# Recurrent gates in four stacked products, weights in a buffer of their own, zero fills spread evenly

## The reference

```python
proj = x @ w_in                                  # B | C | V_A | V_B | G, 512 channels each
y_a = B * conv3(C * V_A)
xc  = conv4(V_B) + bias
r   = sigmoid(einsum('bthi,hij->bthj', xh, wa) + ba)     # xh: xc as 8 heads x 64
i   = sigmoid(einsum('bthi,hij->bthj', xh, wx) + bx)
a   = exp(-8 * r * softplus(-lam)); b = sqrt(1 - a*a) * (i * xc)
h_t = a_t * h_(t-1) + b_t                         # over time
y_b = h * gelu(G)
x1  = layer_norm(alpha * x + concat(y_a, y_b) @ w_out)
y   = layer_norm(alpha * x1 + top-2-of-16 experts(x1))
```

## Time and profile before

| what | value |
|---|---|
| executions timed | 1200.48, 1204.1, 1204.4 us; median 1204.1 |
| the profiled execution | 1197.2 us, of which the span of its instructions is 1195.5 |
| PE busy | 1120.3 us (94% of the span) |
| DVE busy | 808.3 us (68%) |
| ACT busy | 538.6 us (45%) |
| POOL busy | 186.4 us (16%) |
| granted TensorE clock, mean | 0.977 of full speed |

### The profile page before, as it was taken

How to read it: one execution, slowest core, us unless ns; L and a number is a source line. 1 busy time by engine, 2 the same in 40 slices (tenths; PEclk the granted TensorE clock), 3 DMA queues, 4 the chain that set the end, 5 groups by cost and what they waited for, 6 DMA issues and landing times.

```text
span 1195.5 us, 20533 instructions
## 1 busy us (share of the span) xinstructions
PE 1120.3 (94%) x5736; PEld 996.2 (83%) x5737; DVE 808.3 (68%) x1532; ACT 538.6 (45%) x703; POOL 186.4 (16%) x189
## 2 busy tenths in 40 slices
PE   6999999999999999999999988899998999999970
PEld 6999999999999999878888867677887887878750
DVE  5666644465446546767777758797755898888874
ACT  4465433543354336422233312655544676656530
POOL 1000000010001000102222223406101031222222
PEclk9999999999999999999999989899999999999995
DMA  5431368788989454534444225896866789888563
GB/s 188 131 104 50 107 92 121 90 141 128 122 97 133 193 221 164 186 129 159 156 159 141 106 93 184 284 345 219 281 233 240 283 309 369 304 294 293 197 225 143
DMA packets 87274, 221.58 MB, mean 185 GB/s; under 512 B 19152, under 2 KB 45808, under 8 KB 80944
## 3 DMA queue, kind: packets, MB, share of 16 engines
q1 hardware_dynamic: 57824, 129.90, 34.6%
q0 software_dynamic: 18160, 59.53, 15.4%
q10 hardware_dynamic: 11232, 31.47, 13.3%
HBM read 133.75 MB, written 87.11 MB: 185 GB/s over the span
## 4 chain that ended last, share of the span: by engine, by line
PE 71%; DVE 9%; DMA 7%; issue 5%; ACT 4%; DVEq 2%; ACTq 1%; SPq 0%; POOL 0%; POOLq 0%
PE ps_va_b L293 14%; PE ps_vb_c L293 14%; PE ps_h L1488 9%; PE ps_vb_c L907 8%; PE ps_g L293 7%; PE ps_va_b L907 7%; PE ps_o L1466 5%; DMA gate<-g_scr 3%; PE ps_x L1455 2%; PE ps_r_i L302 2%; PE ps_r_i L920 1%; DVE w_lo_p L1658 1%; ACT x_hi L1116 1%; PE ps_h L1517 1%; DMA w_raw<-in_w_out 1%
## 5 line engine op out<-in xcount | busy, mean ns | idle before, releaser
L1488 PE MATMUL ps_h<-x_hi,xt_hi 128*128 x312 | 125.6, 403 | 2.2 <-issue 1.7
L293 PE MATMUL ps_vb_c<-x_hi,w_hi 128*128 (+1 forms) x320 | 114.4, 358 | 9.3 <-DVE x_lo L469 9.3
L1488 PE MATMUL ps_h<-x_hi,xt_lo 128*128 x312 | 121.9, 391 | 0.0
L1488 PE MATMUL ps_h<-w_lo,xt_hi 128*128 x312 | 121.6, 390 | 0.0
L293 PE MATMUL ps_vb_c<-x_hi,w_lo 128*128 (+1 forms) x320 | 113.9, 356 | 0.0
L293 PE MATMUL ps_vb_c<-x_lo,w_hi 128*128 (+1 forms) x320 | 113.2, 354 | 0.0
L293 PE MATMUL ps_va_b<-x_hi,w_lo 128*128 (+1 forms) x320 | 112.7, 352 | 0.0
L293 PE MATMUL ps_va_b<-x_hi,w_hi 128*128 (+1 forms) x320 | 112.6, 352 | 0.0
L293 PE MATMUL ps_va_b<-x_lo,w_hi 128*128 (+1 forms) x320 | 111.8, 349 | 0.0
L543 DVE TENSOR_TENSOR b_t<-a_t 128x420 f32<-128x420 f32 x20 | 11.9, 596 | 95.3 <-ACT a_t L387 95.3
L1121 DVE TENSOR_TENSOR w_lo<-x_hi_p,x_hi 128x2048 f32 (+1 forms) x30 | 68.5, 2288 | 8.5 <-ACT x_hi L1116 6.8
(11 more groups left out here) (361 smaller groups left out, 2680.6 us busy)
## 6 DMA issues: line engine op xcount, KB each, us to landing
x_hi_p<-in_w SPq DMA_DIRECT2D x48, 1024.0 KB, 7.4
o_scr<-x_raw ACTq DMA_DIRECT2D x42, 512.0 KB, 4.9
w_lo_p<-xs_scr SPq DMA_DIRECT2D x41, 512.0 KB, 5.9
o_scr<-w_lo_p SPq DMA_DIRECT2D x41, 512.0 KB, 6.2
w_raw<-in_w_in POOLq DMA_DIRECT2D x19, 512.0 KB, 4.6
xs_scr<-x_raw ACTq DMA_DIRECT2D x18, 512.0 KB, 6.6
x_raw<-in_x_t SPq DMA_DIRECT2D x20, 416.0 KB, 3.4
x_hi_p<-y_scr SPq DMA_DIRECT2D x16, 512.0 KB, 4.3
```

What stands on the lines that cost most here:

```text
L293: mm = pe.matmul(ps[i][:, 0:CHUNK], w[:, i, k], x[:, k, bass.ds(c * CHUNK, CHUNK)], start=(k == 0 and n == 0), stop=(k == KT - 1 and n == 2))
L1488: mm = pe.matmul(ps_h[par][:], x[:, par, k], w[:, bass.ds(at, 1), k].rearrange("p o n -> p (o n)"), start=(k == 0 and n == 0), stop=(k == ...
```

## The change

It has four parts. First, the gates' products: `xc_hi` and `xc_lo` give way to one tile `xc_st` of two slices, one for each head. A slice holds the 64 high rows of its head in one half of the partitions and the 64 low rows in the other. The weights of a slice hold r's block beside i's, and both again below, so a matmul of 128 rows gives hi+lo times the weights, for r and i of one head. With the weights' high and low part that is two matmuls per head, four in all. Head 0's r and i stand in the low and high half of one bank (`ps_ri`), head 1's i and r in those of the other (`ps_ir`); so `xc_hi`, `xc_lo` and the two Tanh become two instructions each, on 64 partitions. Second, the gates' weights come as six pieces instead of one, and for groups 1 to 3 into `l_raw`, columns 1024 to 1279 of `x_raw`, at the head of POOL's loop over the group before. Third, the zero fills: groups 1 and 2 issue seven per step in another order, their last steps five, group 3 four. Fourth, in group 0 every step awaits x by pieces, and SP's late x loads stand between the stores of `y_a` and `y_b`.

```diff
@@ -112,8 +113,7 @@
     xc = sb("xc", [P, LRU_N])
-    xc_hi = sb("xc_hi", [P, LRU_N], F32R)
-    xc_lo = sb("xc_lo", [P, LRU_N], F32R)
+    xc_st = sb("xc_st", [P, 2, LRU_N], F32R)
     ya = sb("ya", [P, EXT + 1])
@@ -127,15 +127,18 @@
     sp_t = sb("sp_t", [P, 8, GROUPS])
-    zero = x_raw[:].rearrange("p a b c -> p (a b c)")[:, 0:D]
+    zero, l_raw = (x_raw[:].rearrange("p a b c -> p (a b c)")[:, a:b] for a, b in ((0, D), (D, D + 2 * P)))
+    l_raw = l_raw.rearrange("p (k n) -> p k n", n=P)
...
     ps_g = ctx.enter_context(nc.psum_tensor("ps_g", [P, 512], F32))
-    ps_vb, ps_c, ps_va, ps_b, ps_r, ps_i = (t[:, i] for t in (ps_vb_c, ps_va_b, ps_r_i) for i in range(2))
+    ps_vb, ps_c, ps_va, ps_b, ps_ri, ps_ir = (t[:, i] for t in (ps_vb_c, ps_va_b, ps_r_i) for i in range(2))
+    low, high = slice(0, HALF), slice(HALF, P)
     ps = [ps_vb, ps_c, ps_va, ps_b, ps_g]
-    mag = ps_r[:, 0:LRU_N]
+    mag = ps_ri[:, 0:LRU_N]
@@ -197,6 +201,14 @@
+    def load_gates(pool, group, to):
+        gate = lambda rows, g, n: w_lru[group, rows, g:g + n, rows].rearrange("o p k n -> p (o k) n")
+        for rows in (low, high):
+            pool.dma_start(to[rows, 0].rearrange("p (k n) -> p k n", n=HALF), gate(low, 0, 2)).then_inc(s_lraw, 16)
+            for g in range(2):
+                pool.dma_start(to[rows, 1:2, (1 - g) * HALF:(2 - g) * HALF], gate(high, g, 1)).then_inc(s_lraw, 16)
     def mix_gpsimd(pool):
@@ -204,18 +216,18 @@
                 pool.wait_ge(s_wlo, i - 1)
-            dst = w_raw[:, i % 2] if i < MT else w_raw[:, i % 2, 0:2]
-            src = w_in[i] if i < MT else w_lru[0]
-            pool.dma_start(dst, src).then_inc(s_wraw[i % 2], 16)
+            if i < MT:
+                pool.dma_start(w_raw[:, i % 2], w_in[i]).then_inc(s_wraw[i % 2], 16)
+            else:
+                load_gates(pool, slice(0, 1), w_raw[:, 1, 0:2])
         with pool.Fori(1, GROUPS) as j:
-            for i in range(WP):
+            for i in range(MT):
                 pool.wait_ge(s_wlo, j * WP + (i - 1))
-                if i < MT:
-                    pool.dma_start(w_raw[:, i % 2],
-                                   w_in[bass.ds(j * MT + i, 1)].rearrange("o p k n -> p (o k) n")).then_inc(s_wraw[i % 2], 16)
-                else:
-                    pool.dma_start(w_raw[:, i % 2, 0:2],
-                                   w_lru[bass.ds(j, 1)].rearrange("o p k n -> p (o k) n")).then_inc(s_wraw[i % 2], 16)
+                pool.dma_start(w_raw[:, i % 2],
+                               w_in[bass.ds(j * MT + i, 1)].rearrange("o p k n -> p (o k) n")).then_inc(s_wraw[i % 2], 16)
+                if i == 1:
+                    pool.wait_ge(s_xlo, NCH * XP)
+                    load_gates(pool, bass.ds(j, 1), l_raw)
         for k in range(KT):
@@ -227,9 +239,11 @@
-        def store_y(j, c, last):
+        def store_y(j, c, last, between=None):
             q = j * NCH + c
             for src, s_ready, s_out, half in ((ya, s_ya, s_ya_out, 0), (yb, s_yb, s_yb_out, GROUPS)):
+                if half and between:
+                    between()
                 sp.wait_ge(s_ready, q + 1)
@@ -245,11 +259,9 @@
         with sp.Fori(0, NCH - 3) as c:
-            store_y(0, c, False)
-            load_x(c + 2, late)
+            store_y(0, c, False, lambda: load_x(c + 2, late))
             load_x(c + 3, early)
-        store_y(0, NCH - 3, False)
-        load_x(NCH - 1, late)
+        store_y(0, NCH - 3, False, lambda: load_x(NCH - 1, late))
         store_y(0, NCH - 2, False)
@@ -278,9 +290,7 @@
             start = isinstance(q, int) and q == 0
-            fresh = isinstance(q, int) and q < 2
-            if not fresh:
-                pe.wait_ge(s_xlo, (c + 1) * XP)
+            fresh = isinstance(j, int) and j == 0
             free = (s_vb, s_c, s_u, s_ya, s_gel)
@@ -297,9 +307,9 @@
                 pe.wait_ge(s_b, q)
-            for g, bank in enumerate((ps_r, ps_i)):
-                for n, (w, x) in enumerate(((l_hi, xc_hi), (l_hi, xc_lo), (l_lo, xc_hi))):
-                    mm = pe.matmul(bank[:, 0:LRU_N], w[:, g], x[:], start=(n == 0), stop=(n == 2))
+            for head, bank in enumerate((ps_ri, ps_ir)):
+                for n, w in enumerate((l_hi, l_lo)):
+                    mm = pe.matmul(bank[:, 0:LRU_N], w[:, head], xc_st[:, head], start=(n == 0), stop=(n == 1))
             mm.then_inc(s_ri, 1)
@@ -310,24 +320,27 @@
-    def raw_piece(i):
-        return (w_raw[:, i % 2], w_hi[:, i], w_lo[:, i]) if i < MT else (w_raw[:, i % 2, 0:2], l_hi[:], l_lo[:])
+    def raw_piece(j, i):
+        gates = w_raw[:, 1, 0:2] if isinstance(j, int) and j == 0 else l_raw
+        return (w_raw[:, i % 2], w_hi[:, i], w_lo[:, i]) if i < MT else (gates, l_hi[:], l_lo[:])
...
-            raw, hi, _ = raw_piece(i)
+            raw, hi, _ = raw_piece(j, i)
             if isinstance(j, int) and j == 0 and i == 0:
                 act.wait_ge(s_w0, 16)
+            elif i < MT:
+                act.wait_ge(s_wraw[i % 2], 16 * (j * (WP // 2 - i % 2) + (i // 2 + i % 2)))
             else:
-                act.wait_ge(s_wraw[i % 2], 16 * (j * (WP // 2) + (i // 2 + i % 2)))
+                act.wait_ge(s_lraw, 16 * 6 * (j + 1))
             act.wait_ge(s_mm[i] if i < MT else s_ri, j * NCH)
...
             if k < KT:
-                act.wait_ge(s_wraw[k % 2], 16 * (W_OUT // 2 + (k // 2 + k % 2)))
+                act.wait_ge(s_wraw[k % 2], 16 * (GROUPS * (WP // 2 - k % 2) + (k // 2 + k % 2)))
                 act.wait_ge(s_mm[MT - 1], READ)
@@ -359,7 +372,8 @@
             act.wait_ge(s_ri, q)
-            act.activation(xc_hi[:], xc[:], ACT.Copy).then_inc(s_xch, 1)
+            act.activation(xc_st[low, 0], xc[low], ACT.Copy)
+            act.activation(xc_st[high, 1], xc[high], ACT.Copy).then_inc(s_xch, 1)
             if split is not None:
@@ -377,9 +391,11 @@
             act.wait_ge(s_h, q)
-            act.activation(a_t[:], ps_r[:, 0:LRU_N], ACT.Tanh, scale=0.5, bias=hrb[:, bass.ds(j, 1)]).then_inc(s_thr, 1)
+            act.activation(a_t[low], ps_ri[low, 0:LRU_N], ACT.Tanh, scale=0.5, bias=hrb[low, bass.ds(j, 1)])
+            act.activation(a_t[high], ps_ir[high, 0:LRU_N], ACT.Tanh, scale=0.5, bias=hrb[high, bass.ds(j, 1)]).then_inc(s_thr, 1)
             act.wait_ge(s_b, q)
-            act.activation(i_t[:], ps_i[:, 0:LRU_N], ACT.Tanh, scale=0.5, bias=hib[:, bass.ds(j, 1)]).then_inc(s_thi, 1)
+            act.activation(i_t[low], ps_ri[high, 0:LRU_N], ACT.Tanh, scale=0.5, bias=hib[high, bass.ds(j, 1)])
+            act.activation(i_t[high], ps_ir[low, 0:LRU_N], ACT.Tanh, scale=0.5, bias=hib[low, bass.ds(j, 1)]).then_inc(s_thi, 1)
             act.wait_ge(s_thr, q + 1)
@@ -420,37 +436,37 @@
                 act.dma_start(g_scr[bass.ds((q * 2 + i) * CAP, P), :], zero[:, 0:1]).then_inc(s_zo, 16)
-                act.dma_start(o_scr[bass.ds((q * 2 + i + (STEPS - NE)) * P, P), :], zero).then_inc(s_zo, 16)
-        def fill_results(q):
-            for i in range(OFILL):
-                act.dma_start(o_scr[bass.ds((q * OFILL + i + STORED) * P, P), :], zero).then_inc(s_zo, 16)
+            fill_results(q, 3, STORED)
+        def fill_results(q, n, first):
+            for i in range(n):
+                act.dma_start(o_scr[bass.ds((q * n + (i + first)) * P, P), :], zero).then_inc(s_zo, 16)
...
             act.dma_start(g_scr[bass.ds(i * P, P), :], zero[:, 0:1]).then_inc(s_zo, 16)
-            act.dma_start(o_scr[bass.ds((i + (STORED + (NCH - 2) * OFILL - 1)) * P, P), :], zero).then_inc(s_zo, 16)
+            fill_results(i - 1, 3, STORED + 3 * (NE // 2))
...
             step(j, NCH - 1, True, lambda i: split_w(j + 1, i), lambda: fill_frozen(j))
...
         with act.Fori(0, NCH - 2) as c:
-            step(GROUPS - 1, c, False, None, lambda: fill_results(c))
+            step(GROUPS - 1, c, False, None, lambda: fill_results(c, 4, STORED + 3 * (NE // 2 + FROZEN)))
         step(GROUPS - 1, NCH - 2, False, lambda i: split_w_out(i) if i < XP else None)
...
-            raw, hi, lo = raw_piece(i)
+            raw, hi, lo = raw_piece(j, i)
             dve.wait_ge(s_whi, j * WP + (i + 1))
@@ -486,7 +502,8 @@
             dve.wait_ge(s_xch, q + 1)
-            dve.tensor_tensor(xc_lo[:], xc[:], xc_hi[:].bitcast(F32), ALU.subtract).then_inc(s_xcl, 1)
+            dve.tensor_tensor(xc_st[high, 0], xc[low], xc_st[low, 0].bitcast(F32), ALU.subtract)
+            dve.tensor_tensor(xc_st[low, 1], xc[high], xc_st[high, 1].bitcast(F32), ALU.subtract).then_inc(s_xcl, 1)
```

More of the change, by code:

```diff
@@ L26 @@
 P = 128
+HALF = P // 2
 D = 1024
@@ L62 @@
 FTAIL = FPAIR + FLAST + 1
-STORED, OFILL = 7, 8
+STORED = 7
 FROZEN = 2
@@ L159, in mixer @@
     s_wraw = [sem(f"s_wraw{i}") for i in range(2)]
+    s_lraw = sem("s_lraw")
     s_xraw = [sem(f"s_xraw{i}") for i in range(2)]
@@ L438, in mix_scalar @@
             step(j, NCH - 1, True, lambda i: split_w(j + 1, i), lambda: fill_frozen(j))
```

(5 more changed lines are left out.)

## The result

The change made the kernel slower: 1210.95 us (median of 8 executions) against 1204.34 (8 executions of the kernel before), ratio 1.0065, 95% interval 1.0048 to 1.0082. In the profiled executions the spans are 1207.3 and 1195.5 us. Of these 11.8 us, 8.1 stand at the first transposes behind the mixer (514.25, now 522.38); the rest of the program is the same, and 7.8 us is what the ratio says. So the place to look is the mixer.

The account below looks back on a forecast made before the run. PE was taken to bound the mixer: products save 7.57 us, ring and weight piece stay hidden, and the end's 8.5 less 1.0 gives -7.5 us, 1196.6 us. Range 1193.5 to 1202, likeliest case 1194.5 to 1199.

Parts of the forecast that it names:

- The products: PE's mixer steps: two matmuls fewer per step, 40 in all, save 7.57 us; a step takes 23.45 us, not 23.83.
- The standstills: DMA nearly stops six or seven us after each g_scr fill; forecast: one standstill of some 8 us instead of two.
- the w_in piece: Third piece of group 2's weights, split in step 9: forecast to land near 247 instead of 251.13, so PE does not wait.
- the second rival: The two g_scr fills are still paid one after the other, the w_in piece stays late; time 1200.9, 2 in 10.
- The price of that rival: PE waits 1.3 to 3.0 us at step 10, a little less at 15, together about 4.3; gain 3.2.
- The ring: ACT and DVE's loop in groups 1 and 2, not through PE: 21.0 us grows to 23.1, between 22.0 and 24.1.
- the third rival: The loop of ACT and DVE exceeds PE's 23.45 us, up to 24.1; gain shrinks some 3 us, to 1199.6; 1 in 10.
- The fourth rival: ACT's full DMA queue holds it some 7 us in each of eight steps; near 1250; 6 in 100 with unseen causes.
- The rule: ACT's fills: 1.24 us per 512 KB, about 0.1 for g_scr, after 0.4 at the start; seven cost 4.4 us.
- The gates' weights: Group 0: six POOL loads instead of one, the last landing 2.7 us later; taken as nothing, bounds 0 and 2.7 us.
- The end of the mixer: Last steps to first transposes: work 8.5 us earlier less 1.0 for two Tanhs, so transposes 7.5 us earlier.
- The loss for the whole: Whole kernel slower by more than about 0.3% (3.6 us): chance 0.07.

Follow-up runs that it names:

- E8: The changed kernel with its seven fills in the order xs g o xs g o o; ratio 1.0112 to the kernel before.
- E10: The changed kernel with each step's second g_scr fill as one 512-byte run, the first still four-byte runs; ratio 0.9942 to the kernel before.
- E1: The changed kernel with each g_scr fill written as one 512-byte run from one partition; ratio 0.9966 to the kernel before.
- E6: The kernel before, six gate matmuls kept, with xc_hi, xc_lo and both Tanhs as two 64-partition instructions each; ratio 1.0163 to the kernel before.
- E4: The changed kernel with the old fills (six per step, old order, eight in group 3); ratio 1.0114 to the kernel before.
- E7: The change, g_scr by 512-byte runs, fills on SP, group 0's gate weights into yb behind the third w_in piece, earlier xc_lo; ratio 0.9958 to before.
- E9: The change, g_scr by 512-byte runs, fills on SP, group 0's gate weights into yb behind the fifth w_in piece, earlier xc_lo; ratio 0.9924 to before.
- E11: The changed kernel with all fills issued by SP instead of ACT, g_scr still as four-byte runs; ratio 0.9943 to the kernel before.
- E5: The kernel before with the new fills alone (seven, five and four, g_scr ahead of o_scr, four-byte runs); ratio 1.0012 to the kernel before.

## Why the prediction was wrong

**The products** were right: 23.45 us a step, and 7.43 us at the last gates' matmuls, where nothing was late.

**The standstills** are the step that failed. I took the two g_scr fills to overlap, as I read the router's four scatters to do, and so had the w_in piece land near 247. It was there at 251.08. They do not overlap: 256 four-byte writes in two fills made two standstills of 6 to 7 us, whether they were issued together (the change) or apart (E8), and one fill made one (E10). It was the second rival, which I gave 2 in 10. The row of the scatters could not carry the reading. At 590 to 592 DMA's busy share is 0.04, that is, it had next to nothing to move, where in a standstill it is 0.3 to 2.1 with transfers waiting; SP issues the next load only then:

```profile
592.00 0.38 SPq L880 DMA_DIRECT2D x_hi_p<-y_scr  x1
```

That load landed 6.8 us after its issue, for a median of 4.3 of its line, so the scatters may have held it for some 2.5 us, not four to six. Besides, a fill writes 128 neighbouring words and the scatters write to different places; whether that matters was not tried. The Trainium skill (DMA: Bandwidth & Descriptors, "Specifications") has transfers under 512 B as read-modify-writes; the traces agree as far as they go: 128 runs of 4 bytes stop the 16 engines for some 6.5 us, one run of 512 bytes does not (E1). That it is a read-modify-write that stops them no run shows.

**The price of that rival** was too small as well: 1.3 to 3.0 us at step 10, "a little less" at 15, where 4.68 and 6.37 came. Two terms were mis-sized. I let PE come 0.8 us earlier against the piece; by its own rows PE is ready for the gates of step 10 about 3 us earlier (275.94 - 4.68 = 271.3, for 274.2 before), what it had gained in all the steps up to there, while the piece landed when it had, since three o_scr fills stood between the second standstill and it instead of one. And the chain behind the piece (from the first gelu step on DVE, 256.81 now and 256.85, to the end of xc_lo, 275.89 and 272.05) grew by 3.9 instead of 3.4. With 2.2 us of slack that makes 3.0 + 3.9 - 2.2 = 4.7. The slower pace of PE behind a wait, 1.6 and 1.9 us, was in no term.

**The ring** came out at 23.5, not 23.1: the Tanhs 1.36 for 1.0, the halves of xc_hi and xc_lo 1.15 for 0.97, the fills 0.13 for 0.1. The terms add up to 23.6; from Tanh to Tanh it is 23.54. That is the third rival, by 0.1 us, and it is why the slack lost at step 10 was not won back: from step 11 to 14 it goes from 1.6 to 0.3 us, where the kernel before had 5 to 6, and step 15 waits longer than step 10. That a half would cost as much as a whole was right (E6), and the lower bound of half was not.

**The fourth rival**, ACT held by its queue, did not come, not even in E8, where its condition was met. The rule that ACT goes on when all but the last two fills are worked off gave nearly the right time for the seven fills of the change (4.4 for 4.60), but by it ACT would have been held through E8's standstill, so the rule is not what happens. What does hold ACT there stays open.

**The gates' weights** in group 0, taken as nothing with bounds to 2.7, cost 0.6 us net, and more in steps 1 and 2: from the first matmul of step 1 (35.60) to that of step 3 (84.28) it is 48.68 us, 1.8 over two steps of 23.45. That step 0 ended 1.2 us earlier than its two matmuls explain (step 1 began at 37.14 before) was luck: the same code began step 1 at 35.51 in E8 and at 37.34 in E1. Where step 1 began near 37, the loss was 0.6 to 1.2 us (E1, E4, E10). Behind the x splits stood the next x loads, and they reached the gates of step 1 and the x of step 2; in E7 and E9 the loss is gone.

**The end of the mixer** follows its own sum where the mixer is clear of waits: the transposes of E9 come 6.95 us earlier than before, for the 7.5 forecast. The last w_out load lands 8.5 us earlier, as forecast (478.72, for 487.25), and the chain behind it grew by 1.6 instead of 1.0, of which 1.4 are the Tanhs. E9 has its fills on SP, though, so that the 8.5 agrees is in part luck. The dip of the clock at the transposes was taken to shift unchanged; from the first group of transposes to the second it is 15.8 us in E9, for 15.1 before.

**The loss for the whole** was given 7 in 100, nearly all of it for another mechanism. Each term was looked at against its own cover; that the same 2.4 us at step 10 had to cover three of them, and PE's gain as well, was seen, but then the landing of one piece was left to decide, by an argument from the scatters.

## What to carry to other kernels

When PE becomes faster, what is tied to a DMA does not come along: set PE's whole gain up to that place against the slack there, not one step's. An instruction on half the partitions cost as much here as one on all, so a product that saves two matmuls (0.38 us) and splits four instructions of the other engines (2.5 us) only pays where these have time. Fill a column of memory as one long run, and from a queue whose engine is idle: E1 and E11 change one thing each, and either turns this change from a loss into a gain.

## What the runs showed of the hardware

Half-partition Tanhs in a row stand 0.62 us apart, whole ones 0.50: the halves overlap less, so two cost 1.24 us for one of 0.50 (E6, with the old products, has the same 0.62).

A fill of 512 bytes in four-byte runs costs DMA about 6.5 us, five times what a 512 KB fill takes (1.3 us at the 404 GB/s of E1). The packet records of the change have most of the 128 writes of step 8's second fill between 230.2 and 230.8, ahead of the first standstill, and the other transfers stand still behind them. E1 also reads the 512 bytes from one partition instead of 128, so whether it is the writes or the reads that stop DMA is not shown.

And a wait of 4 us costs PE more than 4 us, since the granted clock is then at its lower level for some 3 us of work. The length of the wait alone does not tell: a wait of 1.47 us in E5 cost 0.1 us beside itself (276.48 to 300.42 is 23.94 for 23.83), one of 2.26 us in E6 0.2 (403.96 to 429.76, less the next wait of 1.73, is 24.07), and one of 1.99 us in E4 1.65 (274.21 to 299.31 is 25.10 for 23.45).
